# Weight ring of a two-block transformer kernel: w_down_2's pieces at byte 0 of their slot, all others at byte 16, slots 64 bytes longer

## What is computed

```python
def conv_gated_mlp(h, w_up, conv_w, conv_b, w_down):
    up = h @ w_up
    up = causal_depthwise_conv(up, conv_w) + conv_b
    gate, val = jnp.split(up, 2, axis=-1)
    return (jax.nn.silu(gate) * val) @ w_down        # w_down: 5632 x 2048
```

## Time and profile before

| | before |
|---|---|
| median of 3 runs | 2663.68 us (2663.10 to 2665.05) |
| the profiled execution | 2666.81 us, with a span of 2665.0 us |
| PE busy | 2587.0 us, 97% of the span, 19024 matmuls |
| PE weight loads busy | 2417.4 us, 91% |
| DVE busy | 1658.2 us, 62% |
| ACT busy | 1139.6 us, 43% |
| DMA, mean over the span | 206 GB/s |
| instructions | 42761 |

### The profile page before, as it was taken

One profiled execution on the slowest core, in us unless ns is written; L12 is line 12 of the kernel. 1 busy time (PEld: TensorE's weight loads), 2 busy tenths in 40 slices (PEclk: granted clock), 3 DMA queues, 4 the chain that ended last, 5 costly groups with the idle time before them and its releaser, 6 DMA issues.

```text
span 2665.0 us, 42761 instructions
## 1 busy us (share of the span) xinstructions
PE 2587.0 (97%) x19024; PEld 2417.4 (91%) x19024; DVE 1658.2 (62%) x1989; ACT 1139.6 (43%) x1293; POOL 11.2 (0%) x24
## 2 busy tenths in 40 slices
PE   6799999999998999999999999999899999999998
PEld 4478799789997999999999999899899889988996
DVE  4266566557786754555555568966667647764775
ACT  3332555534435443434434454044445435543544
POOL 0000000000000000000000000000000000000000
PEclk9899999999998999999999999999999999999999
DMA  9776555567875765555555555445355555555553
GB/s 373 303 265 238 193 202 206 175 219 283 300 292 186 285 208 188 190 188 182 186 188 190 176 178 200 145 158 189 131 190 181 199 188 190 179 201 190 190 178 121
DMA packets 77225, 547.77 MB, mean 206 GB/s; under 512 B 8849, under 2 KB 8977, under 8 KB 12273
## 3 DMA queue, kind: packets, MB, share of 16 engines
q1 hardware_dynamic: 74304, 533.53, 56.9%
q0 software_dynamic: 2448, 11.01, 1.1%
q10 hardware_dynamic: 288, 0.50, 0.1%
HBM read 539.77 MB, written 5.24 MB: 205 GB/s over the span
## 4 chain that ended last, share of the span: by engine, by line
PE 92%; DMA 3%; DVE 3%; ACT 2%; issue 1%; SPq 0%; POOL 0%; DVEq 0%; ACTq 0%
PE acc L286 22%; PE acc L284 22%; PE acc L288 22%; PE acc L304 5%; PE acc L305 5%; PE acc L306 5%; PE acc L341 4%; DMA raw<-in_w_mod 2%; PE mp L304 1%; PE mp L306 1%; PE mp L305 1%; PE mp L371 1%; DVE macc L415 1%; PE mp L1820 1%; DVE wlo L252 0%
## 5 line engine op out<-in xcount | busy, mean ns | idle before, releaser
L252 DVE TENSOR_TENSOR wlo<-raw,whi 128x1024 fp32r<-128x1024 f32 x781 | 945.1, 1223 | 733.4 <-ACT whi L242 730.8
L242 ACT ACTIVATE whi<-raw 128x1024 fp32r<-128x1024 f32 x781 | 819.8, 1058 | 1220.5 <-PE acc L288 906.0
L284 PE MATMUL acc<-hh,whi 128*128 128x256 f32 x3360 | 946.9, 282 | 13.5 <-DVE wlo L252 7.8
L286 PE MATMUL acc<-hl,whi 128*128 128x256 f32 x3360 | 939.1, 279 | 0.0
L288 PE MATMUL acc<-hh,wlo 128*128 128x256 f32 x3360 | 935.6, 278 | 0.0
L284 PEld LDWEIGHTS acc<-hh,whi 128*128 128x128 f32 x3360 | 633.1, 188 | 19.9 <-issue 13.4
L286 PEld LDWEIGHTS acc<-hl,whi 128*128 128x128 f32 x3360 | 634.6, 189 | 1.4 <-issue 1.0
L288 PEld LDWEIGHTS acc<-hh,wlo 128*128 128x128 f32 x3360 | 631.9, 188 | 0.0
L286 PE MATMUL acc<-ml,whi 128*128 128x256 f32 x1536 | 431.1, 281 | 0.0
L284 PE MATMUL acc<-mh,whi 128*128 128x256 f32 x1536 | 428.3, 279 | 1.6 <-DVE wlo L252 1.6
L288 PE MATMUL acc<-mh,wlo 128*128 128x256 f32 x1536 | 427.0, 278 | 0.0
(11 more groups left out here) (310 smaller groups left out, 2219.0 us busy)
## 6 DMA issues: line engine op xcount, KB each, us to landing
raw<-in_w_in SPq DMA_DIRECT2D x98, 1024.0 KB, 4.9
raw<-in_w_mod SPq DMA_DIRECT2D x96, 1024.0 KB, 5.4
raw<-in_w_up SPq DMA_DIRECT2D x88, 1024.0 KB, 4.9
raw<-in_w_mlp_in SPq DMA_DIRECT2D x64, 1024.0 KB, 4.9
raw<-in_w_mlp_out SPq DMA_DIRECT2D x64, 1024.0 KB, 4.9
raw<-in_w_down SPq DMA_DIRECT2D x44, 1024.0 KB, 4.9
raw<-in_w_out SPq DMA_DIRECT2D x32, 1024.0 KB, 5.0
raw<-in_w_fourier_out SPq DMA_DIRECT2D x8, 1024.0 KB, 5.2
```

Of the source, the lines that this page charges most:

```text
L242: nc.scalar.activation(whi[:, r, :], raw_slot(k)[:, 2 * GC * j:2 * GC * (j + 1)], ACT.Copy)\
L252: nc.vector.tensor_tensor(wlo[:, r, :], raw_slot(k)[:, 2 * GC * j:2 * GC * (j + 1)], whi[:, r, :].bitcast(f32), ALU.subtract).then_inc(S[" ...
L284: nc.tensor.matmul(dst, whi[:, r, cols], hi[:, kt, :], start=begin, stop=False, skip_group_check=True)
L286: nc.tensor.matmul(dst, whi[:, r, cols], lo[:, kt, :], start=False, stop=False, skip_group_check=True)
```

## The change

`whi` and `wlo` become tensors of four slots of 2 x 512 + 16 elements (4160 bytes each instead of 4096). A list `TOKEN` marks 88 of the 781 pieces, those of `w_down_2`. The new helper `ring(part, p)` gives the piece's view in its slot: from element 0 for a marked piece, from element 4 (16 bytes) for any other. ACT, DVE and PE use it in place of `whi[:, r, ...]` and `wlo[:, r, ...]`. No instruction is added, removed or moved, and no semaphore changes. Each tensor grows by 192 bytes, so `wlo` starts at 65920 instead of 65728 and all that comes after it lies 384 bytes further on; 192 and 384 are multiples of 64.

```diff
--- before.py
+++ after.py
@@ -71,6 +71,11 @@
               [8, 9, 14, 15], [10, 11, 16, 17], [0, 1, 2, 3], [4, 5]]
 
 
+TOKEN = [False] * len(PIECE)
+for _end, _n in ((len(PIECE) - 168, 32), (len(PIECE) - 72, 32), (len(PIECE), 24)):
+    TOKEN[_end - _n:_end] = [True] * _n
+
+
 def late_groups(p):
 
     return max(0, STREAM[:PIECE[p - 1][0]].count("m") - EARLY) // 4
@@ -107,8 +112,8 @@
 
 
         raw = sb("raw", [P, NSLOT, 4 * GC])
-        whi = sb("whi", [P, 8 * GC + 16], f32r)[:, 4:8 * GC + 4].rearrange("p (r n) -> p r n", r=4)
-        wlo = sb("wlo", [P, 8 * GC + 16], f32r)[:, 4:8 * GC + 4].rearrange("p (r n) -> p r n", r=4)
+        whi = sb("whi", [P, 4, 2 * GC + 16], f32r)
+        wlo = sb("wlo", [P, 4, 2 * GC + 16], f32r)
         tmp = sb("tmp", [P, 2, 4 * NT])
         (mrow, cv, posc, macc, stage, _, posc2, sx, post) = overlay(
             "region_s", 8192,
@@ -232,14 +237,18 @@
         def raw_slot(k):
             return raw[:, RING[k], :] if RING[k] < NSLOT else raw2[:, RING[k] - NSLOT, :]
 
+        def ring(part, p):
+
+            off = 0 if TOKEN[p] else 4
+            return part[:, p % 4, off:off + 2 * GC]
+
         def hi_piece(act, st):
             k, j = PIECE[st.p]
-            r = st.p % 4
             if j == 0:
                 slot_in(act, k)
             if st.p >= 4:
                 act.wait_ge(S["used"], st.p - 3)
-            nc.scalar.activation(whi[:, r, :], raw_slot(k)[:, 2 * GC * j:2 * GC * (j + 1)], ACT.Copy)\
+            nc.scalar.activation(ring(whi, st.p), raw_slot(k)[:, 2 * GC * j:2 * GC * (j + 1)], ACT.Copy)\
                 .then_inc(S["hi_n"], 1)
             st.p += 1
@@ -247,10 +256,9 @@
             k, j = PIECE[st.p]
             while EARLY <= st.m < EARLY + LATE and MSLOT[st.m] < k:
                 mod_acc(dve, st)
-            r = st.p % 4
             dve.wait_ge(S["hi_n"], st.p + 1)
-            nc.vector.tensor_tensor(wlo[:, r, :], raw_slot(k)[:, 2 * GC * j:2 * GC * (j + 1)],
-                                    whi[:, r, :].bitcast(f32), ALU.subtract).then_inc(S["lo_n"], 1)
+            nc.vector.tensor_tensor(ring(wlo, st.p), raw_slot(k)[:, 2 * GC * j:2 * GC * (j + 1)],
+                                    ring(whi, st.p).bitcast(f32), ALU.subtract).then_inc(S["lo_n"], 1)
             st.p += 1
 
         def conv_hi(act, st, n=8, met=None):
...
@@ -273,7 +281,7 @@
 
         def feature_piece(pe, st, i, hi, lo, k0, nkt=KT, w=GC):
 
-            r = st.p % 4
+            wh, wl = ring(whi, st.p), ring(wlo, st.p)
             pe.wait_ge(S["lo_n"], st.p + 1)
             for k in range(2 * GC // w):
                 kt = k0 + k
@@ -281,11 +289,11 @@
                     dst = acc[i][:, t * NT:(t + 1) * NT]
                     cols = slice(k * w + t * P, k * w + (t + 1) * P)
                     begin = kt == 0 and t % 2 == 0
-                    nc.tensor.matmul(dst, whi[:, r, cols], hi[:, kt, :], start=begin, stop=False,
+                    nc.tensor.matmul(dst, wh[:, cols], hi[:, kt, :], start=begin, stop=False,
                                      skip_group_check=True)
-                    nc.tensor.matmul(dst, whi[:, r, cols], lo[:, kt, :], start=False, stop=False,
+                    nc.tensor.matmul(dst, wh[:, cols], lo[:, kt, :], start=False, stop=False,
                                      skip_group_check=True)
-                    last = nc.tensor.matmul(dst, wlo[:, r, cols], hi[:, kt, :], start=False,
+                    last = nc.tensor.matmul(dst, wl[:, cols], hi[:, kt, :], start=False,
                                             stop=kt == nkt - 1, skip_group_check=True)
             last.then_inc(S["used"], 1)
             st.p += 1
...
@@ -295,15 +303,15 @@
             outs = [(acc[i], 0, *both, 0), (acc[i], GC, *both, P)]
             if ctx_bank:
                 outs += [(ctx_bank, 0, ch, cl, 0), (ctx_bank, GC, ch, cl, P)]
-            r = st.p % 4
+            wh, wl = ring(whi, st.p), ring(wlo, st.p)
             pe.wait_ge(S["lo_n"], st.p + 1)
             for k in range(2):
                 kt, cols = k0 + k, slice(k * GC, (k + 1) * GC)
                 for bank, off, hi, lo, t0 in outs:
                     dst = bank[:, off:off + GC]
-                    nc.tensor.matmul(dst, hi[:, kt, t0:t0 + P], whi[:, r, cols], start=kt == 0, stop=False)
-                    nc.tensor.matmul(dst, hi[:, kt, t0:t0 + P], wlo[:, r, cols], start=False, stop=False)
-                    last = nc.tensor.matmul(dst, lo[:, kt, t0:t0 + P], whi[:, r, cols], start=False,
+                    nc.tensor.matmul(dst, hi[:, kt, t0:t0 + P], wh[:, cols], start=kt == 0, stop=False)
+                    nc.tensor.matmul(dst, hi[:, kt, t0:t0 + P], wl[:, cols], start=False, stop=False)
+                    last = nc.tensor.matmul(dst, lo[:, kt, t0:t0 + P], wh[:, cols], start=False,
                                             stop=kt == nkt - 1)
             last.then_inc(S["used"], 1)
             st.p += 1
...
```

More of the change, by code:

```diff
@@ L355, in mm_lr @@
                     dst = acc[i][0:LRW, x * GC:x * GC + NT]
-                    nc.tensor.matmul(dst, whi[:, r, cols], hi[:, kt, :], start=kt == 0, stop=False)
-                    nc.tensor.matmul(dst, whi[:, r, cols], lo[:, kt, :], start=False, stop=False)
-                    last = nc.tensor.matmul(dst, wlo[:, r, cols], hi[:, kt, :], start=False, stop=kt == KT - 1)
+                    nc.tensor.matmul(dst, wh[:, cols], hi[:, kt, :], start=kt == 0, stop=False)
+                    nc.tensor.matmul(dst, wh[:, cols], lo[:, kt, :], start=False, stop=False)
+                    last = nc.tensor.matmul(dst, wl[:, cols], hi[:, kt, :], start=False, stop=kt == KT - 1)
             last.then_inc(S["used"], 1)
```

## The result

The changed kernel takes 2684.21 us (median of 4 runs, 2683.90 to 2686.74) against 2664.36 us for the kernel before (4 runs, 2663.10 to 2668.09): a ratio of 1.0071, with a 95% interval of 1.0058 to 1.0085. Its profiled execution took 2686.74 us.

What follows compares the result with a forecast made beforehand. PE, busy nearly throughout, was taken to bound the kernel by the distance between matmul starts. The terms -1.9, 0 and 0 us, applied to a median of 2663.7 us, gave 2661.8 us, range 2653 to 2673.

Steps and rivals of the forecast that it cites:

- What bounds the kernel: Whole kernel: PE, busy 97% of the span, sets the time, so the distance between matmul starts is what counts.
- Part 1: w_down_2's 88 pieces moved to byte 0: 1.8 ns less for each of 1056 matmuls, 1.9 us of gain.
- Part 2: The 693 pieces staying at byte 16, with a pitch of 4160 bytes: places modulo 64 kept, cost 0.
- (d): Features after the first two w_down_2 stages go at the slow pace: 6.2 us lost, 2669.9 us, at most 2674.8; chance 0.17.
- if the pace of the other 10,000 matmuls changes: Stated sign that the prediction fails: matmuls other than those moved to byte 0 change pace; no size given.
- Part 3: ACT and DVE at the ring's new starts: still 1058 and 1223 ns a piece, hidden behind PE, cost 0.
- (a): w_down_2's moved pieces: no effect, a start at 16 costs no more than at 0; 2663.7 us, chance 0.18.
- (b): w_down_2's moved pieces save a stretch of 64 bytes, 7.2 ns a matmul: 7.6 us gained, 2656.1 us; chance 0.17.
- (c): Matmuls against dh: shifted starts slow float32r streams, aligned ones take 215.6 ns; 17.8 us less, 2645.9 us; chance 0.13.
- (e): Slow feature stretches from 879 to 1895 us go quick: at least 12.6 us gained, 2651.1 us; chance 0.05.

Runs made afterwards that it cites:

- e1: The changed kernel with the `TOKEN` list empty: slots of 4160 bytes, but every piece at byte 16; 2687.32 us, ratio 1.0098.
- e3: The kernel before, pitch still 4096 bytes, with 79 of w_down_2's pieces at byte 0 and a longer ScalarE wait for three pieces behind a stage; 2661.32 us.
- e8: The kernel before with unused tensors that move `wlo` 64 and the activations 256 bytes further on; ratio 1.0004.
- f3: The kernel before with `wlo` 64 and the activations 256 bytes further on, and 79 of w_down_2's pieces at byte 0; ratio 0.9997.
- e5: The kernel before with 256 unused bytes between `wlo` and `tmp`, so the activations lie 256 bytes further on; ratio 0.9994.
- e4: The kernel before with 384 unused bytes between `wlo` and `tmp`, so the activations lie 384 bytes further on; ratio 1.0066.
- e6: The kernel before with 128 unused bytes between `wlo` and `tmp`, so the activations lie 128 bytes further on; ratio 1.0066.
- e7: The kernel before with unused tensors that move `wlo` 192 and the activations 256 bytes further on; ratio 1.0114.
- g1: The same kernel as f3, run again for another profile; ratio 1.0002, profiled run 2671.00 us.
- e9: The kernel before with unused tensors that move `wlo` 128 and the activations 256 bytes further on; ratio 1.0031.

## Why the prediction was wrong

It forecast 2661.8 us, a range of 2653 to 2673, and gave slower 0.17. The time came out 11 us above the range.

**What bounds the kernel** held: PE without idle time, distances between starts as the measure, 232.5 ns against dh.

**Part 1** met the size, by luck. Forecast: 1.8 ns a matmul less, the middle between 0 and 3.6. Measured: 1.4 to 1.5 ns (e1 against the change: 232.5 to 231.1; e3 alone: 231.3), about 1.5 us, which no time here tells from nothing. But how it was reached, by stretches of 32 bytes, is not borne out: by slot the changed kernel has 228.5, 230.2, 232.8 and 233.0 ns where e1, with the offset of 16, has 231.2, 231.3, 232.9 and 234.6, so the gain is 2.8, 1.0, 0.1 and 1.6 ns, and in e8's arrangement it is 0.1. The gain of a piece goes by its slot and arrangement, so a single price for the offset was the wrong form.

**Part 2 is the step that failed.** It put the term of the 693 pieces left at byte 16 at 0; the runs showed some 21 us (19.9 us of longer span, and 1.5 us gained against dh). It costed them at 0 because their place modulo 64 is kept, and gave as proof that "whi and wlo already differ so before and keep the same distances". That proof was no proof: L286 and L288 run in one loop, whose pace shows what the whole arrangement costs, and never what one line alone does. Taken one by one in the trace of before, the matmuls behind L284, L286 and L288 start 117.5, 118.3 and 117.5 ns after them in the middle, and 119.2, 114.2 and 113.3 ns at the end, with the same operands. The kernel before has only one D and one E, so nothing in its trace could tell how the pace goes with them. The modulus of 64 rests on no row. What should have been weighed was the shift of `wlo` by 192 bytes and of everything behind it by 384, of which the prediction keeps only that they are multiples of 64, and the two paces of the earlier trace rows: 2.3 ns for all of the 15,500 feature matmuls is 36 us, not the 6.2 us of rival (d). Even that is a scale and no bound, since 119.8 and 120.0 ns stand in no row of before. The prediction's own sign of failure, "if the pace of the other 10,000 matmuls changes", is what came, and as a loss it had been given no chance and no price.

**Part 3** held: 1057 and 1223 ns a piece, cover as before.

**The rivals.** (d) had the right kind of mechanism (PE settles in a slower pace), the wrong place and price: it named 2688 matmuls behind the w_down_2 stages, the loss is in all features and the first of it before 1662 us. Nor is it the known slow pace (117.8): PE doesn't settle in one of two, but takes four new ones by slot (118.1 to 119.8, mean 118.8), in the middle and at the end alike, so the sum of (d) was bounded by a row that was no bound. (a), by which the start at 16 costs nothing, is off by 1.5 ns a matmul for the pieces moved. Starts that differ by multiples of 64 bytes move a feature matmul between 115.6 and 120.0 ns. The Trainium skill, page "SBUF — State Buffer", section "Specifications (TRN2)", speaks only of lines of 16 bytes, of hits in them and crossings between them, and by that all those starts are alike; the measurement disagrees with it as a full account. (b) and (c), one stretch of 64 bytes or the whole excess, are refuted: in no slot of any arrangement is the mean against dh under 228.4 ns, where (b) wanted 225 and (c) 215.6. (e), the quick pace in the middle, didn't occur in the changed kernel; e8 and f3 have it there in their quick runs, at other places than the change gives.

## What to carry to other kernels

A change of a tensor's length moves all that is allocated behind it, and where PE is without idle time that can be worth more than the edit itself: here two tensors of 192 bytes more, with nothing else changed, cost 38 us (e2), while the offset that was meant is worth some 1.5, too little to be seen in the time. Add up the starts of the operands modulo 256 before and after, and keep their distances with a filler (in e5, 256 bytes gave the paces of before to 0.1 ns). A view over one line of a loop gives the loop's pace; two lines that agree there prove nothing about either operand.

## What the runs showed of the hardware

- Float32r matmuls of 256 columns with 128 columns of weights loaded for each follow each other in 115.6 to 120.0 ns (means over a stage) at a granted clock of 1.00, by the places of the operands modulo 256 bytes. Float32 matmuls (L341) keep 216 ns in the kernels before and after, whose places differ.
- The same places allow several paces, each kept for hundreds of microseconds: 117.8 and 115.6 ns (before), 117.8 and 120.0 (e4, e6), 117.3 and 120.0 (e7), 115.8, 117.8 and 118.5 (f3, g1). Where an arrangement has several, the runs of one program spread: 2651 to 2673 us for f3, against 2667 to 2674 for e9, whose profile shows 117.8 ns in every stage.
- Moving `wlo` by 64, 128 or 192 bytes, with `whi` and the activations kept in place modulo 256, changes the pace (e7, e8, e9). This changes its distance to `whi` and its distance to the stream together, and no run parts the two. That the reading of the stream and the loading of the next weights get into each other's way would fit all of it with the distances to the stream alone, but no run took one of them away: it is argued, not shown. Open is also what decides which pace PE settles in, and whether distances modulo more than 256, or in steps finer than 64, matter too: only multiples of 64 were tried for the features.
